# Attention pieces at two places of a dense tile, and the scores of two heads on halves of TensorE's rows

## The chip, the cores and the metric

One core of one Trainium2 chip runs the whole program in one launch. The time is the device time of one execution in microseconds (us); lower is better. The time of the kernel before is 2365.88 us, the median of three runs (2365.64, 2365.88 and 2370.18).

## The reference, cut to what matters

Two layers work on 256 tokens of width 1024. In each layer one input projection feeds three mixers of 8 heads of width 64 each. A is attention with 8 query heads on 2 key heads, with a position bias and learned sinks; B is attention with a cumulative forget bias; C is stick-breaking attention. Their outputs are projected, gated, added and projected once more. A layer ends with an expert stage of 16,384 one-neuron experts.

```python
h = rms_norm(x, norm1_g[l]) * (1.0 + sc1) + sh1
x = x + g1 * parallel_mixers(h, w_in[l], ...)
h = rms_norm(x, norm2_g[l]) * (1.0 + sc2) + sh2
x = x + g2 * peer_ffn(h, w_query[l], ...)
# A: s = q k / 8 - slope * dist, softmax with a sink in the denominator
# B: s = q k / 8 + F[t] - F[s], F = cumsum(log f), causal softmax
# C: beta = sigmoid(q k / 8); A[t,s] = beta[t,s] * prod_{s<j<t} (1 - beta[t,j])
```

## The kernel before

**Weight tiles.** All weights come as a stream of tiles of 128 x 1024 float32, one DMA each (L349), into four buffers `raw`. ScalarE copies a tile to the rounded type fp32r as `hi` (`head`, L445), VectorE computes the rest `lo` = raw - hi (`rest_of`, L751), and TensorE multiplies three times for each of a tile's eight chunks (`product`, L1230 to L1234): hi by mov_hi, hi by mov_lo, lo by mov_hi, 256 columns each. So a tile is 24 matmuls. `rest_of` runs AHEAD = 3 tiles before the tile that TensorE is at; `head` of tile t + 3 waits until tile t - 1 is done (L444).

**The dense stage.** A layer begins with DENSE = 55 tiles: 31 give the queries, keys, values and forget gates of A, B and C, and 24 the merge gates. Results go to two PSUM banks `pj` in turn, from where ScalarE takes them to `projT` (`evict`, L495, L499). The attention of the three mixers is cut into pieces that are issued between these tiles, at numbers written out by hand at L83 to L89. Each engine has its own loop over the tile number t:

- TensorE (L1381 to L1449) issues first all pieces of t and then the tile's 24 matmuls. Pieces are `scores` for one head (L1293; two heads at each t of 8 to 11 for A and of 20 to 23 for B), `turn` (transposes of the probabilities, L1315), `values` (L1324), `logits` of one head of C (L1334), `tails` (L1347), `stick_values` (L1362), and `norms`, `turn_v`, `turn_y`.
- VectorE (L914 to L975) issues first `rest_of` of tile t + 3 and then its pieces: `biased` (L825: two reductions from PSUM at L834 per head), `prob_copy` (L851), `divided` (L860), `normed` (L819), for C `stick_parts` (L875), `stick_arg_of` (L888) and `stick_mask` (L895), and at 24 numbers ADA_AT a `modulation` (L756), a pass over a 512 KB tile of other weights with its own DMA (L357).
- ScalarE (L555 to L596) issues `head` of t + 3, its pieces (`softplus` of C, L518, three passes of 384 columns), and `evict` of t.

Mixer C takes one head at each number of STICK: TensorE does `logits` at t, ScalarE `softplus` at t, VectorE `stick_parts` at t + 1, TensorE `tails` at t + 2 (it waits for L885, the last instruction of `stick_parts`), VectorE `stick_arg_of` at t + 2 and `stick_mask` at t + 3, TensorE `stick_values` at t + 5. Heads use two places of `stick`, and the banks 0, 1 and 2, 3 of `wk`, in turn.

**Scores.** A head's queries and keys lie on 64 partitions: rows 0 to 63 or 64 to 127 of the array. `scores` and `logits` multiply float32 operands, which the profile shows as two matmul passes per instruction. For B the forget bias is added by two fp32r matmuls with 8 rows each (L1311, L1312), after each of the two score matmuls:

```python
for q0, nk, c0 in ((0, P, 0), (P, 2 * P, P)):
    last = pe.matmul(s[:, c0:c0 + nk], q[:, q0:q0 + P], k[:, 0:nk], start=True, stop=br == 0)
    if br:
        pe.matmul(s[:, c0:c0 + nk], pick_f, f_hi[:, 0:nk], start=False, stop=False)
        last = pe.matmul(s[:, c0:c0 + nk], pick_f, f_lo[:, 0:nk], start=False, stop=True)
```

`scores` of a head waits until VectorE has read the head two before (`score_read`), since two banks are used in turn.

Of the kernel before, what the change touches and what calls it, by code (L numbers as in the profile page):

```python
# [20 lines left out]
P = 128  # L21
KC = D // P
HD = 64
# [74 lines left out]
C_ID, C_ONE, C_IOTA, C_ZERO, C_EPS, C_C = 0, 128, 256, 384, 385, 386  # L98
NCONST = 386 + KC
# [5 lines left out]
def trunk(nc, stream, par_dram, const_dram, mix_dram, taba_dram, keys_dram, front_dram, ada_dram, x_dram, out_dram):  # L105
# [4 lines left out]
    with ctx:  # L110
# [19 lines left out]
        picks = sb("picks", [HEADS, HEADS], f32r)  # L130
# [6 lines left out]
        f_pair = routes  # L137
# [75 lines left out]
        f_hi, f_lo = f_pair[0:HEADS, 0, :], f_pair[0:HEADS, 1, :]  # L213
# [58 lines left out]
        f_ready = sem("f_ready")  # L272
        score_ready = sem("score_ready")
# [165 lines left out]
        def _(act):  # L439
# [19 lines left out]
            with act.Fori(0, DEPTH) as l:  # L459
# [95 lines left out]
                for t in range(DENSE):  # L555
# [32 lines left out]
                    if t in STICK:  # L588
                        softplus(STICK.index(t))
                    if t - 2 in STICK:  # L590
                        stick_tail(STICK.index(t - 2))
# [147 lines left out]
        def _(dve):  # L739
# [28 lines left out]
            nc.vector.tensor_copy(picks[:, :], ident[0:HEADS, 0:HEADS])  # L768
# [8 lines left out]
            with dve.Fori(0, DEPTH) as l:  # L777
# [136 lines left out]
                for t in range(DENSE):  # L914
                    rest_of(L0 + (t + AHEAD), t + AHEAD)
# [11 lines left out]
                    if t == SCORE_A + 1:  # L927
# [7 lines left out]
                        link(nc.vector.tensor_scalar(f_hi, fl[:, 2, :], -1.0, None, ALU.mult))  # L935
                        nc.vector.scalar_tensor_tensor(f_lo, fl[:, 2, :], -1.0, f_hi.bitcast(f32), ALU.mult,
                                                       ALU.subtract).then_inc(f_ready, 1)
                    if t == SCORE_A + 3:
                        maxima(0, 1)
                    if TURN_A <= t < TURN_A + 4:  # L940
                        prob_copy(0, 2 * (t - TURN_A))
                        prob_copy(0, 2 * (t - TURN_A) + 1)
# [15 lines left out]
                    if TURN_B <= t < TURN_B + 4:  # L958
                        prob_copy(1, 2 * (t - TURN_B))
                        prob_copy(1, 2 * (t - TURN_B) + 1)  # L960
# [4 lines left out]
                    if t - 2 in STICK:  # L965
# [263 lines left out]
        def _(pe):  # L1229
# [21 lines left out]
            with pe.Fori(0, DEPTH) as l:  # L1251
# [9 lines left out]
                def project(t, j, o, bank, chunks=None, at=range(KC)):  # L1261
# [31 lines left out]
                def scores(br, h):  # L1293
                    n = 8 * br + h

                    if n >= 2:
                        pe.wait_ge(score_read, 16 * l + n - 1)
                    if br == 0:
                        o = (h // 4) * HD
                        q, k = projT[o:o + HD, QA + h % 4, :], projT[o:o + HD, KA, :]  # L1300
                    else:
                        o = (h % 2) * HD
                        q, k = projT[o:o + HD, QB + h // 2, :], projT[o:o + HD, KB + h // 2, :]
                    s = wk[:, 2 + h % 2, :]
                    pick_f = picks[0:HEADS, h:h + 1].to_broadcast([HEADS, P])
# [18 lines left out]
                def values(br, h):  # L1324
                    pe.wait_ge(pt_copied, 16 * l + 8 * br + h + 1)
                    v = (h // 4) * HD if br == 0 else P + h * HD
# [7 lines left out]
                def logits(h):  # L1334
                    if h >= 2:
                        pe.wait_ge(z_read, 8 * l + h - 1)
                    else:

                        pe.wait_ge(score_read, 16 * l + 16)
                    o = (h % 2) * HD  # L1340
# [40 lines left out]
                for t in range(DENSE):  # L1381
# [10 lines left out]
                    if SCORE_A <= t < SCORE_A + 4:  # L1392
                        scores(0, 2 * (t - SCORE_A))
                        scores(0, 2 * (t - SCORE_A) + 1)
                    if VALUE_A <= t < VALUE_A + 4:
                        values(0, 2 * (t - VALUE_A))
                        values(0, 2 * (t - VALUE_A) + 1)
                    if TURN_A <= t < TURN_A + 4:
                        turn(0, 2 * (t - TURN_A))
                        turn(0, 2 * (t - TURN_A) + 1)  # L1400
# [11 lines left out]
                    if t == SCORE_B:  # L1412
                        pe.wait_ge(out_free, l * OUTS + (VB + 4 + 2))
# [15 lines left out]
                    if t == V_C:  # L1429
                        pe.wait_ge(out_free, l * OUTS + (VC + 4 + 2))  # L1430
                        pe.wait_ge(y_read, 3 * l + 2)
                        turn_v(VC, 4, 4)
                    if t == STICK[0]:
                        pe.wait_ge(out_free, l * OUTS + (KCT + 4 + 2))
                    if t == STICK[0] + 5:
                        pe.wait_ge(vtok_in, 3 * l + 3)
                    if t - 5 in STICK:
                        stick_values(STICK.index(t - 5))
# [227 lines left out]
```

## Time and profile before

| what | value |
| --- | --- |
| median of three runs | 2365.88 us |
| the profiled execution, its own time | 2368.43 us |
| span of its instructions | 2366.5 us |
| TensorE matmul busy | 2260.6 us (96%) |
| VectorE busy | 1658.2 us (70%) |
| ScalarE busy | 1225.9 us (52%) |
| mean granted TensorE clock | 0.975 of full speed |
| DMA | 427.46 MB, 181 GB/s in the mean |

PE is TensorE's matmuls, PEld its weight loads, DVE is VectorE, ACT ScalarE, POOL GpSimd, SP SyncE. Matmuls are pipelined: their ends are modelled and their durations overlap, so the time of one is read from start to start. PEclk is the granted clock as a share of full speed: 1.00 is 2.4 GHz, 0.50 is 1.2 GHz. Idle time stands behind the bar or in brackets, with the instruction that ended it.

### The profile page before, as it was taken

The page shows a single profiled execution, that of the slowest core. Times are in us where ns is not written, and L with a number is a line of the kernel's source. Part 1 is how long each engine was busy: PE and PEld are TensorE (multiplying, and loading weights), DVE is VectorE, ACT ScalarE, POOL GpSimd, SP SyncE. Part 2 cuts the span into 40 slices and gives each one's busy share as a digit, 9 for nine tenths or more (in the row PEclk, how much of TensorE's full clock was granted, in tenths as well). Part 3 has the DMA queues.
Part 4 walks back from the last instruction along what each step waited for, and adds up shares of the span by engine and source line. Part 5 has one row for each costly group of instructions (what it writes and reads, how often), then busy time and mean ns, then how long its engine had stood idle before and what let it go on. Part 6 is the DMA issues. An engine that isn't in the chain of part 4 may idle for free.

```text
span 2366.5 us, 45922 instructions
## 1 busy us (share of the span) xinstructions
PE 2260.6 (96%) x15348; PEld 2097.7 (89%) x15348; DVE 1658.2 (70%) x3147; ACT 1225.9 (52%) x2136; POOL 229.6 (10%) x266
## 2 busy tenths in 40 slices
PE   5998998999999999999989999999999999999998
PEld 4888998999999988888878889889999999888887
DVE  6645574788869966777556556738887799567765
ACT  4444545444557755554454445454445677555454
POOL 0000000000037700000000000000001475000000
PEclk7989999999999999999999899999999999999999
DMA  8434553455553357887644345435555433577764
GB/s 320 150 132 165 188 182 125 160 179 185 170 174 110 116 168 239 253 263 229 194 168 156 120 175 190 167 116 178 186 171 193 143 116 107 195 254 254 261 215 160
DMA packets 114451, 427.46 MB, mean 181 GB/s; under 512 B 12704, under 2 KB 12960, under 8 KB 113056
## 3 DMA queue, kind: packets, MB, share of 16 engines
q1 hardware_dynamic: 114336, 426.08, 53.8%
q8 instruction: 54, 0.88, 0.1%
q14 instruction: 61, 0.50, 0.1%
HBM read 424.98 MB, written 1.05 MB: 180 GB/s over the span
## 4 chain that ended last, share of the span: by engine, by line
PE 90%; DVE 3%; issue 3%; ACT 2%; DMA 1%; SPq 0%; ACTq 0%; DVEq 0%
PE pj L1232 17%; PE pj L1233 16%; PE pj L1234 16%; PE wk L1232 10%; PE wk L1234 10%; PE wk L1233 10%; PE wk L1524 5%; PE wk L1307 1%; ACT hi L445 1%; DMA arena<-in_front 1%; PE wk L1494 1%; PE wk L1257 1%; PE wk L1281 0%; PE wk L1343 0%; PE wk L1321 0%
## 5 line engine op out<-in xcount | busy, mean ns | idle before, releaser
L751 DVE TENSOR_TENSOR lo<-raw,hi 128x1024 fp32r<-128x1024 f32 x683 | 839.2, 1230 | 646.3 <-ACT hi L445 637.8
L1232 PE MATMUL pj<-mov_hi,hi 128*128 128x256 f32 x3376 | 993.8, 294 | 39.8 <-DVE mov_lo L802 26.2
L1233 PE MATMUL pj<-mov_lo,hi 128*128 128x256 f32 x3376 | 967.6, 287 | 0.0
L1234 PE MATMUL pj<-mov_hi,lo 128*128 128x256 f32 x3376 | 966.6, 286 | 0.0
L445 ACT ACTIVATE hi<-raw 128x1024 fp32r<-128x1024 f32 x683 | 720.5, 1056 | 454.7 <-PE wk L1234 344.7
L1232 PEld LDWEIGHTS pj<-mov_hi,hi 128*128 128x128 f32 x3376 | 659.2, 195 | 51.7 <-DVE mov_lo L802 28.8
L1233 PEld LDWEIGHTS pj<-mov_lo,hi 128*128 128x128 f32 x3376 | 661.1, 196 | 0.5
L1234 PEld LDWEIGHTS pj<-mov_hi,lo 128*128 128x128 f32 x3376 | 659.8, 195 | 0.0
L1232 PE MATMUL wk<-hi,mov_hi 128*128 128x512 f32 x1024 | 398.6, 389 | 1.7 <-DVE mov_lo L1181 1.7
L1234 PE MATMUL wk<-hi,mov_lo 128*128 128x512 f32 x1024 | 398.4, 389 | 0.0
L1233 PE MATMUL wk<-lo,mov_hi 128*128 128x512 f32 x1024 | 398.3, 389 | 0.0
L433 POOL TENSOR_SCALAR mov_hi<-const,routes 128x128 fp32r<-128x128 f32 x256 | 218.2, 868 | 1188.8 <-DVE gateT L1133 1059.5
L1232 PEld LDWEIGHTS wk<-hi,mov_hi 128*128 128x128 f32 x1024 | 192.2, 188 | 41.9 <-DVE mov_lo L1181 2.1
L1234 PEld LDWEIGHTS wk<-hi,mov_lo 128*128 128x128 f32 x1024 | 192.2, 188 | 39.9
L1233 PEld LDWEIGHTS wk<-lo,mov_hi 128*128 128x128 f32 x1024 | 192.2, 188 | 39.9
L649 ACT ACTIVATE arena<-pj 128x256 f32 (+1 forms) x192 | 73.5, 384 | 276.0 <-PE pj L1234 275.9
L1145 DVE TENSOR_SCALAR onehot_a<-const,routes,gateT 128x128 f32<-128x128 f32 x512 | 147.0, 351 | 0.0
L756 DVE SCALAR_TENSOR_TENSOR arena<-arena,silu_c 128x1024 f32<-128x1024 f32 x88 | 106.4, 1219 | 2.4 <-DMA arena<-in_front 2.2
L1181 DVE TENSOR_TENSOR mov_lo<-arena,mov_hi 128x256 fp32r<-128x256 f32 x256 | 106.5, 417 | 1.1 <-ACT mov_hi L711 1.1
L711 ACT ACTIVATE mov_hi<-arena 128x256 fp32r (+1 forms) x256 | 102.3, 401 | 0.0
L495 ACT ACTIVATE arena<-pj 128x256 f32<-128x256 f32 x62 | 23.8, 383 | 150.5 <-PE pj L1234 150.5
L676 ACT ACTIVATE mov_lo<-const,routes 128x128 fp32r<-128x128 f32 x256 | 81.0, 397 | 0.0
(182 smaller groups left out, 1597.4 us busy)
## 6 DMA issues: line engine op xcount, KB each, us to landing
raw<-in_stream SPq DMA_DIRECT2D x684, 512.0 KB, 3.4
arena<-in_ada SPq DMA_DIRECT2D x72, 512.0 KB, 4.6
onehot_a<-in_ada SPq DMA_DIRECT2D x24, 512.0 KB, 4.6
arena<-in_front SPq DMA_DIRECT2D x4, 2048.0 KB, 18.0
arena<-in_taba SPq DMA_DIRECT2D x2, 1536.0 KB, 19.0
arena<-in_keys SPq DMA_DIRECT2D x2, 1024.0 KB, 4.7
x<-in_xT SPq DMA_DIRECT2D x1, 1024.0 KB, 4.8
arena<-in_mix SPq DMA_DIRECT2D x2, 512.0 KB, 15.2
```

The costliest lines, as they stand in the source:

```text
L433: e = nc.gpsimd.tensor_scalar(onehot_b[0][:, quad % 4 * 2 + r, :], iota, idx2T[:, t:t + 1], None, ALU.is_equal)
L445: nc.scalar.activation(hi[j % SPLIT][:, :], raw[j % RAW][:, :], ACT.Copy).then_inc(hi_done, 1)
L676: e = nc.scalar.activation(onehot_b[1][:, slot + r, :], iota, ACT.Abs, bias=idx2T[:, quad * 4 + r:quad * 4 + r + 1], scale=-1.0)
L711: nc.scalar.activation(w_hi[:, s, :], group_of(n), ACT.Copy).then_inc(w_head, 1)
L751: nc.vector.tensor_tensor(lo[j % SPLIT][:, :], raw[j % RAW][:, :], hi[j % SPLIT][:, :].bitcast(f32), ALU.subtract).then_inc(lo_done, 1)
L756: nc.vector.scalar_tensor_tensor(tile, tile, 1.0, silu_c[:, :], ALU.mult, ALU.mult, accum_out=col)\
L1145: e = nc.vector.tensor_scalar(onehot_a[:, quad % 2 * 4 + r, :], iota, idx1T[:, t:t + 1], gateT[:, t:t + 1], ALU.is_equal, ALU.mult)
L1181: nc.vector.tensor_tensor(w_lo[:, s, :], group_of(n), w_hi[:, s, :].bitcast(f32), ALU.subtract).then_inc(w_rest, 1)
L1232: pe.matmul(out, w_h, m_h, start=first, stop=False)
L1233: pe.matmul(out, w_h, m_l, start=False, stop=False)
L1234: return pe.matmul(out, w_l, m_h, start=False, stop=last)
L1524: last = pe.matmul(wk[:, 2 + quad % 4, :].rearrange("p (i t) -> p t i", t=4)[:, r, :], onehot_a[:, quad % 2 * 4 + r, :], onehot_b[half][:, ...
```

## The change

It gives the pieces two places per tile. In TensorE's loop `early_pieces` go ahead of the tile (norms, scores, tails, logits, transposes of values of A and C and of the outputs), and `late_pieces` after the tile's fourth chunk of eight (turns, values, the transposes of B's values, stick values). In VectorE's loop all pieces but `prob_copy` and `modulation` now stand ahead of `rest_of`. Mixer C takes two heads at each of four numbers of STICK, the second head of a pair one tile behind the first on ScalarE and VectorE, with `stick_values` four tiles behind instead of five. ADA_AT is drawn anew.

`scores` and `logits` take a pair of heads, one on rows 0 to 63 and the other on rows 64 to 127, each to its own bank, and their matmuls stand side by side: both heads' first 128 queries, then both heads' rest. For B the forget bias is added by one fp32r matmul of 64 rows per head and part, where rows 0 to 7 and 64 to 71 of `f_rows` hold the rounded part and rows 32 to 39 and 96 to 103 the remainder, and the other rows are zeros that GpSimd writes. The heads of A are renumbered so that a pair uses both key heads. The layout of weights on the host follows.

```diff
-STICK = (27, 29, 32, 34, 37, 39, 42, 44)
-V_C, Y_C = 31, 50
+STICK = (28, 33, 38, 43)
+V_C, Y_C = 31, 49
 SIGMOID = (47, 49)
-ADA_AT = (5, 13, 14, 16, 18, 19, 22, 24, 25, 27, 29, 31, 32, 34, 36, 39, 41, 42, 44, 46, 48, 49, 51, 53)
+ADA_AT = (5, 13, 14, 18, 20, 21, 22, 24, 25, 26, 27, 31, 32, 33, 36, 37, 41, 42, 46, 47, 50, 51, 52, 53)
...
+                wait_alone(pool, sq_ready, 2 * KC * l + KC)
+                nc.gpsimd.memset(f_rows.bitcast(f32), 0.0).then_inc(f_zero, 1)
...
                 for t in range(DENSE):
-                    rest_of(L0 + (t + AHEAD), t + AHEAD)
+                    for n in range(2):
+                        if t - n - 1 in STICK:
+                            stick_parts(2 * STICK.index(t - n - 1) + n)
+                        if t - n - 3 in STICK:
+                            stick_mask(2 * STICK.index(t - n - 3) + n)
+                    for n in range(2):
+                        if t - n - 2 in STICK:
+                            stick_arg_of(2 * STICK.index(t - n - 2) + n)
...
+                        dve.wait_ge(f_zero, l + 1)
+                        nc.vector.tensor_scalar(f_rows[64:64 + HEADS, :], fl[:, 2, :], -1.0, None, ALU.mult)
+                        link(nc.vector.tensor_scalar(f_rows[0:HEADS, :], fl[:, 2, :], -1.0, None, ALU.mult))
+                        for at in (32, 96):
+                            e = nc.vector.scalar_tensor_tensor(f_rows[at:at + HEADS, :], fl[:, 2, :], -1.0,
+                                                               f_rows[0:HEADS, :].bitcast(f32), ALU.mult, ALU.subtract)
+                        e.then_inc(f_ready, 1)
...
-                    if t - 3 in STICK:
-                        stick_mask(STICK.index(t - 3))
-                    if t - 2 in STICK:
-                        stick_arg_of(STICK.index(t - 2))
-                    if t - 1 in STICK:
-                        stick_parts(STICK.index(t - 1))
...
+                    rest_of(L0 + (t + AHEAD), t + AHEAD)
+                    if TURN_A <= t < TURN_A + 4:
+                        prob_copy(0, 2 * (t - TURN_A))
+                        prob_copy(0, 2 * (t - TURN_A) + 1)
+                    if TURN_B <= t < TURN_B + 4:
+                        prob_copy(1, 2 * (t - TURN_B))
+                        prob_copy(1, 2 * (t - TURN_B) + 1)
                     if t in ADA_AT:
                         modulation(ADA_AT.index(t))
                 rest_of(L0 + (DENSE + AHEAD), DENSE + AHEAD)
...
                         if chunks is not None:
                             pe.wait_ge(mov_ready, l * M_READY + (chunks + k + 1))
+                        if between is not None and k == KC // 2:
+                            between()
                         last = product(pj[bank][:, 0:SEQ], *chunk(j, k), mov_hi[:, at[k], :], mov_lo[:, at[k], :],
...
+                    n = 8 * br + 2 * pair
+                    if n % 8:
+                        pe.wait_ge(score_read, 16 * l + n)
                     for q0, nk, c0 in ((0, P, 0), (P, 2 * P, P)):
-                        last = pe.matmul(s[:, c0:c0 + nk], q[:, q0:q0 + P], k[:, 0:nk], start=True, stop=br == 0)
+                        for h in range(2):
+                            rows = slice(h * HD, (h + 1) * HD)
+                            q = projT[rows, (QA, QB)[br] + pair, q0:q0 + P]
+                            k = projT[rows, KA if br == 0 else KB + pair, 0:nk]
+                            last = pe.matmul(wk[:, 2 + h, c0:c0 + nk], q, k, start=True, stop=br == 0)
                         if br:
-                            pe.matmul(s[:, c0:c0 + nk], pick_f, f_hi[:, 0:nk], start=False, stop=False)
-                            last = pe.matmul(s[:, c0:c0 + nk], pick_f, f_lo[:, 0:nk], start=False, stop=True)
-                    last.then_inc(score_ready, 1)
+                            for h in range(2):
+                                rows = slice(h * HD, (h + 1) * HD)
+                                last = pe.matmul(wk[:, 2 + h, c0:c0 + nk],
+                                                 picks[rows, 2 * pair + h:2 * pair + h + 1].to_broadcast([HD, P]),
+                                                 f_rows[rows, 0:nk], start=False, stop=True)
+                    last.then_inc(score_ready, 2)
...
-                def logits(h):
-                    if h >= 2:
-                        pe.wait_ge(z_read, 8 * l + h - 1)
+                def logits(pair):
+                    if pair:
+                        pe.wait_ge(z_read, 8 * l + 2 * pair)
                     else:
                         pe.wait_ge(score_read, 16 * l + 16)
-                    o = (h % 2) * HD
-                    q, k = projT[o:o + HD, QC + h // 2, :], projT[o:o + HD, KCT + h // 2, :]
-                    z = wk[:, 2 + h % 2, :]
-                    pe.matmul(z[:, 0:SEQ], k[:, 0:P], q, start=True, stop=True)
-                    pe.matmul(z[:, SEQ:SEQ + P], k[:, P:2 * P], q[:, P:2 * P], start=True,
-                              stop=True).then_inc(z_ready, 1)
+                    for n, (q0, nq, c0) in enumerate(((0, SEQ, 0), (P, P, SEQ))):
+                        for h in range(2):
+                            rows = slice(h * HD, (h + 1) * HD)
+                            q, k = projT[rows, QC + pair, q0:q0 + nq], projT[rows, KCT + pair, n * P:(n + 1) * P]
+                            last = pe.matmul(wk[:, 2 + h, c0:c0 + nq], k, q, start=True, stop=True)
+                    last.then_inc(z_ready, 2)
                 def tails(h):
...
+                def early_pieces(t):
...
+                def late_pieces(t):
+                    if VALUE_A <= t < VALUE_A + 4:
+                        values(0, 2 * (t - VALUE_A))
+                        values(0, 2 * (t - VALUE_A) + 1)
+                    if TURN_A <= t < TURN_A + 4:
+                        turn(0, 2 * (t - TURN_A))
+                        turn(0, 2 * (t - TURN_A) + 1)
...
-                        pe.wait_ge(qk_done, 2 * l + 2)
-                        pe.wait_ge(f_ready, l + 1)
-                    if SCORE_B <= t < SCORE_B + 4:
-                        scores(1, 2 * (t - SCORE_B))
-                        scores(1, 2 * (t - SCORE_B) + 1)
...
+                    for n in range(2):
+                        if t - n - 4 in STICK:
+                            stick_values(2 * STICK.index(t - n - 4) + n)
...
+                for t in range(DENSE):
+                    early_pieces(t)
+                    project(L0 + t, t, t, t % 2, None if t else 0, between=lambda: late_pieces(t))\
+                        .then_inc(tile_done, 2 if t == DENSE - 1 else 1)
...
+            if b == "a":
+                wo = wo.reshape(8, HD, D)[qh].reshape(512, D)
```

## Rows read from the trace of the kernel before

**Rows 1.** The page's busy time: us, share of the span, and instructions of each engine.

```profile
PE 2260.6 (96%) x15348; PEld 2097.7 (89%) x15348; DVE 1658.2 (70%) x3147; ACT 1225.9 (52%) x2136; POOL 229.6 (10%) x266
```

**Rows 2.** Waits of TensorE, whole run: us in total, times, longest.

```profile
PE wk L1356 <- DVE arena L885: 22.3, 16, 2.8
...
PE wk L1307 <- DVE arena L822: 3.6, 4, 1.3
PE wk L1377 <- DVE arena L869: 3.2, 2, 1.6
...
PE wk L1329 <- DVE arena L858: 1.4, 2, 0.7
...
PE wk L1290 <- ACT arena L495: 0.9, 2, 0.5
```

**Rows 3.** The dense stages of layers 1 and 2: busy, PEclk, DMA share, GB/s.

```profile
39.50:297.10 257.60, 241.82 (x1764) 227.44 (x1763) 148.09 (x258) 123.84 (x228) 5.59 (x3) 0.94 0.47 160
1204.50:1461.70 257.20, 241.47 (x1766) 227.46 (x1766) 148.86 (x260) 124.28 (x229) 5.60 (x3) 0.94 0.46 160
```

**Rows 4.** Timeline of VectorE, one head of mixer C: start, us, instruction [idle before].

```profile
230.44 1.23 DVE L751 TENSOR_TENSOR lo<-raw,hi 128x1024 fp32r<-128x1024 f32 x1 [2.84 <-ACT hi L445]
...
232.64 0.55 DVE L885 SCALAR_TENSOR_TENSOR arena<-wk,arena 128x384 f32<-128x384 f32 x1
```

**Rows 5.** Stretches at and before a drop of the clock, columns as in rows 3.

```profile
68.90:72.30 3.40, 3.40 (x18) 3.40 (x17) 0.52 (x4) 0.00 (x0) 0.00 (x0) 0.50 0.51 154
126.90:130.30 3.40, 3.40 (x17) 2.28 (x17) 2.25 (x10) 0.02 (x1) 1.07 (x1) 1.00 0.80 301
130.30:133.70 3.40, 3.40 (x19) 3.40 (x18) 0.34 (x2) 0.00 (x0) 0.00 (x0) 0.51 0.67 243
...
1427.40:1430.80 3.40, 1.51 (x13) 1.31 (x13) 3.37 (x6) 1.42 (x2) 0.00 (x0) 1.00 0.40 136
1430.80:1434.20 3.40, 3.40 (x19) 3.40 (x18) 2.31 (x4) 0.53 (x1) 0.00 (x0) 0.50 0.92 320
```

**Rows 6.** Timeline of TensorE, two products of a tile inside 130.30:133.70.

```profile
130.70 0.41 PE L1232 MATMUL pj<-mov_hi,hi 128*128 128x256 f32 x1
130.91 0.41 PE L1233 MATMUL pj<-mov_lo,hi 128*128 128x256 f32 x1
```

**Rows 7.** Timeline of TensorE, one head's `scores` of B and the next head's start.

```profile
143.94 0.50 PE L1307 MATMUL wk<-arena 64*128 64x128 f32 x2
...
145.78 0.37 PE L1307 MATMUL wk<-arena 64*128 64x128 f32 x1
```

**Rows 8.** Timeline of TensorE, two heads' `scores` of A, the tile before, the turns after.

```profile
81.82 0.28 PE L1233 MATMUL pj<-mov_lo,hi 128*128 128x256 f32 x1
81.94 0.28 PE L1234 MATMUL pj<-mov_hi,lo 128*128 128x256 f32 x1
82.14 1.57 PE L1307 MATMUL wk<-arena 64*128 64x128 f32 x8
83.65 0.66 PE L1321 MATMUL wk<-const,arena 128*128 128x128 f32 x4
```

**Rows 9.** Timeline of TensorE, the last `values` of B, `logits` of one head of C.

```profile
174.66 0.39 PE L1330 MATMUL wk<-arena 128*128 128x64 f32 x2
174.88 0.39 PE L1331 MATMUL wk<-arena 128*128 128x64 f32 x2
175.20 0.70 PE L1343 MATMUL wk<-arena 64*128 64x256 f32 x2
...
176.04 0.39 PE L1232 MATMUL pj<-mov_hi,hi 128*128 128x256 f32 x1
```

**Rows 10.** Groups of VectorE's instructions by form in 42:297: busy us, mean ns.

```profile
L756 DVE SCALAR_TENSOR_TENSOR onehot_a<-onehot_a,silu_c 128x1024 f32<-128x1024 f32 x12 | 14.6, 1218 | 0.0
...
L834 DVE CUSTOM_DVE_ANT_0 arena<-wk,arena 128x256 f32<-128x256 f32 x16 | 6.7, 417 | 0.0
```

**Rows 11.** The page's DMA issues: count, KB each, us from issue to landing.

```profile
onehot_a<-in_ada SPq DMA_DIRECT2D x24, 512.0 KB, 4.6
```

More of the change, by code:

```diff
@@ L96 @@
 NPAR = 102
-C_ID, C_ONE, C_IOTA, C_ZERO, C_EPS, C_C = 0, 128, 256, 384, 385, 386
-NCONST = 386 + KC
+C_ID, C_ONE, C_IOTA, C_EPS, C_C, C_PICK = 0, 128, 256, 384, 385, 385 + KC
+NCONST = 385 + KC + HEADS
 X_BLK, X_TRI, X_CM, X_BT = 0, 128, 256, 640
@@ L129, in trunk @@
         silu_c = sb("silu_c", [P, D])
-        picks = sb("picks", [HEADS, HEADS], f32r)
+        picks = sb("picks", [P, HEADS], f32r)
         mod = sb("mod", [P, N_ADA])
@@ L212, in trunk @@
         fl = sq[0:HEADS, 5:8, :]
-        f_hi, f_lo = f_pair[0:HEADS, 0, :], f_pair[0:HEADS, 1, :]
+        f_rows = routes[:, 0, :]
         pj = [ctx.enter_context(nc.psum_tensor(f"pj{i}", [P, 512], f32)) for i in range(2)]
@@ L272, in trunk @@
         f_ready = sem("f_ready")
+        f_zero = sem("f_zero")
         score_ready = sem("score_ready")
@@ L587, in _ @@
                         v_copy(2, wk[:, 4:6, :], P + 512, P + 1024)
-                    if t in STICK:
-                        softplus(STICK.index(t))
-                    if t - 2 in STICK:
-                        stick_tail(STICK.index(t - 2))
+                    for n in range(2):
+                        if t - n in STICK:
+                            softplus(2 * STICK.index(t - n) + n)
+                        if t - n - 2 in STICK:
+                            stick_tail(2 * STICK.index(t - n - 2) + n)
                     if t == SIGMOID[0]:
@@ L767, in _ @@
             dve.wait_ge(setup_loaded, 32)
[L768 removed]
+            nc.vector.tensor_copy(picks[:, :], const[:, C_PICK:C_PICK + HEADS])
             dve.sem_inc(x_ready, KC)
@@ L1259, in squares, with project @@
                         last.then_inc(ss_ready, 1)
-                def project(t, j, o, bank, chunks=None, at=range(KC)):
+                def project(t, j, o, bank, chunks=None, at=range(KC), between=None):
                     pe.wait_ge(lo_done, t + 1)
@@ L1291, in turn_v, with scores @@
                     last.then_inc(vtr, 1)
[L1293 to L1301, printed above, removed]
[L1302 to L1313 removed]
+                def scores(br, pair):
+                    n = 8 * br + 2 * pair
+                    if n % 8:
+                        pe.wait_ge(score_read, 16 * l + n)
+                    for q0, nk, c0 in ((0, P, 0), (P, 2 * P, P)):
+                        for h in range(2):
[3 more added lines that the diff above has]
+                            last = pe.matmul(wk[:, 2 + h, c0:c0 + nk], q, k, start=True, stop=br == 0)
+                        if br:
+                            for h in range(2):
[4 more added lines that the diff above has]
+                    last.then_inc(score_ready, 2)
                 def turn(br, h):
@@ L1379, in turn_y @@
                         last.then_inc(ytr, 1)
-                for t in range(DENSE):
+                def early_pieces(t):
                     if t == NORM_A + 1:
@@ L1392, in _ @@
                     if SCORE_A <= t < SCORE_A + 4:
[L1393 to L1400, printed above, removed]
+                        scores(0, t - SCORE_A)
                     if t == NORM_BQ:
@@ L1412, in _ @@
                     if t == SCORE_B:
+                        pe.wait_ge(qk_done, 2 * l + 2)
+                        pe.wait_ge(f_ready, l + 1)
+                    if SCORE_B <= t < SCORE_B + 4:
+                        scores(1, t - SCORE_B)
+                    if t == V_C:
+                        pe.wait_ge(out_free, l * OUTS + (VC + 4 + 2))
+                        pe.wait_ge(y_read, 3 * l + 2)
+                        turn_v(VC, 4, 4)
+                    for n in range(2):
+                        if t - n - 2 in STICK:
+                            tails(2 * STICK.index(t - n - 2) + n)
+                    if t == STICK[0]:
+                        pe.wait_ge(out_free, l * OUTS + (KCT + 4 + 2))
+                    if t in STICK:
+                        logits(STICK.index(t))
+                    if t == Y_C + 2:
+                        pe.wait_ge(stick_arg, 8 * l + 8)
+                        turn_y(1, 0)
+                    if t == Y_C + 3:
+                        pe.wait_ge(z_read, 8 * l + 8)
+                        turn_y(2, 2)
+                def late_pieces(t):
[5 more added lines that the diff above has]
+                        turn(0, 2 * (t - TURN_A) + 1)
+                    if t == SCORE_B:
                         pe.wait_ge(out_free, l * OUTS + (VB + 4 + 2))
@@ L1428, in _ @@
                         turn(1, 2 * (t - TURN_B) + 1)
[L1429 to L1435, printed above, removed]
-                        pe.wait_ge(vtok_in, 3 * l + 3)
-                    if t - 5 in STICK:
-                        stick_values(STICK.index(t - 5))
-                    if t - 2 in STICK:
-                        tails(STICK.index(t - 2))
-                    if t in STICK:
-                        logits(STICK.index(t))
-                    if t == Y_C + 2:
-                        pe.wait_ge(stick_arg, 8 * l + 8)
-                        turn_y(1, 0)
-                    if t == Y_C + 3:
-                        pe.wait_ge(z_read, 8 * l + 8)
-                        turn_y(2, 2)
-                    project(L0 + t, t, t, t % 2, None if t else 0).then_inc(tile_done, 2 if t == DENSE - 1 else 1)
+                    if t == STICK[0] + 4:
+                        pe.wait_ge(vtok_in, 3 * l + 3)
+                    for n in range(2):
+                        if t - n - 4 in STICK:
[4 more added lines that the diff above has]
+                        .then_inc(tile_done, 2 if t == DENSE - 1 else 1)
                 for n in range(N_BR):
@@ L1618, in _lay_out @@
         q[:, PQP] = i["q_norm_peer"][l]
-        q[:, PSINK:PSINK + 8] = i["sinks"][l]
+        q[:, PSINK:PSINK + 8] = i["sinks"][l][qh]
         q[0:8, PBF] = i["b_forget"][l]
@@ L1639, in _lay_out @@
     taba = np.zeros((P, HEADS, 384), np.float32)
-    for h in range(HEADS):
+    for n, h in enumerate(qh):
         s = 2.0 ** -(h + 1)
         a, b = own - s * d_own, prev - s * d_prev
-        taba[:, h] = np.concatenate([a, b, a], 1)
+        taba[:, n] = np.concatenate([a, b, a], 1)
     keys = np.zeros((DEPTH, P, PEER_HEADS, 256), np.float32)
```

16 lines of the change are left out of this document (3 added, 13 removed).

## The prediction

> **What bounds the kernel now.** The page comes first: TensorE has matmuls in flight 96% of the span, VectorE 70%, ScalarE 52% [rows 1]. So the bound is TensorE's row, and time can leave it in three ways: less work, less idle time, a higher clock. The change touches only the two dense stages, so I read those in the windows: 257.6 and 257.2 us, with VectorE busy 148 to 149 us and ScalarE 124 us [rows 3]. The 55 tiles alone, 24 matmuls each with starts 0.12 us apart [rows 8], are 55 x 2.88 = 158 us. The other 99 us per layer are pieces, idle time and low clock.
>
> The waits of TensorE name the idle time [rows 2]: 22.3 us for `stick_parts` ahead of `tails` (16 times, all heads of C in both layers), 3.6 us for `normed`, 3.2 for `divided`, 1.4 for `prob_copy`, and 0.9 for the eviction of a tile whose values are to be turned. VectorE's timeline shows why [rows 4]: it sat idle 2.84 us until `head` was done, spent 1.23 us on the weight split, and only then began `stick_parts`, whose last instruction starts 2.20 us after the split's start. The pieces stand behind a split that TensorE needs three tiles later.
>
> The clock is the third loss. After a stretch of 3.4 us with only 1.51 us of matmuls the granted clock is 0.50 for the next 3.4 us, and the same follows a stretch that was busy throughout but with `scores` of B [rows 5]. At that level the products start 0.21 us apart instead of 0.12 [rows 6, 8], so of such a stretch a share of 1 - 0.12/0.21 = 0.43 is lost. In the two stages, after their first tile, the clock drops eleven times, first at 68.9 us and last at 1430.8 [rows 5], seven times for 3.4 us and four times for 6.8: 51.2 us. Six drops follow a stretch with idle time (27.3 us, two of them long), the other five a stretch with `scores` of B (23.9 us).
>
> **The change part by part**, as savings against the profiled execution's own 2368.43 us.
>
> *Pieces ahead of the split.* `stick_parts` may now start as soon as ScalarE's logarithms are there, beside the `head` of the same tile, so it uses the 2.84 us in which VectorE idled. It ends some 2.2 us into its tile, and `tails` comes at the next tile, at least 2.88 us after. `normed` and `divided` move ahead of the split likewise and `values` move 12 matmuls (1.44 us) later than the tile's start, more than the waits' 1.3, 1.6 and 0.7 us. So 22.3 + 3.6 + 3.2 + 1.4 = 30.5 us go. The 0.9 us stay: the eviction is bound to the tile's end. What is late next is the second head of a C pair, whose `stick_parts` waits for a `softplus` that itself comes behind `head`; it has 0.5 to 1 us to spare. I allow 2 us of new waits: **28.5 us**, between 20 and 30.5.
>
> What now stands behind these pieces is `rest_of` of t + 3, with the DMA that refills its `raw` buffer (SyncE waits for the split), and the `head` of t + 4. A split that comes 2 to 3 us later still ends some two tiles, over 5 us, ahead of its products. SyncE's queue is passed by nothing new: the modulations' DMAs follow the refills as before. But four modulations stand at 24 to 27 and at 50 to 53. Each one's buffer is refilled after the split one tile earlier and lands 4.6 us later [rows 11], against tiles of 2.9 to 4.9 us, so VectorE can stand still 1 to 2 us there, behind `prob_copy` and behind the split. I cost it at nothing: the cover is the splits' lead. Without it, it would be 2 to 4 us per layer. The same holds for GpSimd's fill of `f_rows` and two more writes of 8 rows on VectorE.
>
> *Drains in B.* One head's `scores` of B take 145.78 - 143.94 = 1.84 us [rows 7], two heads of A 83.65 - 82.14 = 1.51 us [rows 8]. The float32 work is the same, so B's forget bias costs 3.68 - 1.51 = 2.17 us per pair for eight small matmuls. Their columns would be 4 x 0.11 + 4 x 0.12 = 0.92 us. The rest is the change from 64 rows to 8 and back; a change of rows from 128 to 64 shows the same, since `logits` starts at 175.20 where the passes before it end their step at 174.88 + 0.22 = 175.10 [rows 9]. The new form has four bias matmuls per pair of 64 rows, so no change of rows: 1.51 + 0.46 = 1.97 us against 3.68, a saving of 1.71 per pair, for 8 pairs **13.7 us**. If the cost lay in the change between float32 and fp32r, only half the matmuls would be saved, 8 x 0.46 = 3.7 us; that is the lower end.
>
> *Logits.* One head takes 176.04 - 175.10 = 0.94 us [rows 9], two 1.88. A pair in one place has the columns of a pair of A, 1.51. 8 x 0.37 = **3.0 us**.
>
> *Two heads side by side.* No row has two neighbouring matmuls on different halves, so this is bounded: nothing at one end, half of the float32 passes at the other. A head's two passes share their rows and cannot overlap, so of the order 0, 0, 1, 1 each second pass of a head can run beside the first of the other: five steps instead of eight, 0.87 us instead of 1.30 (passes of 0.11 and 0.22 us). The weight loads say the same: passes with 64 columns start 0.11 us apart [rows 9], no faster than passes with 128, so a pass needs 0.11 us for its weights however short it is, and eight make 0.88 us. That is 0.43 us for each of 24 pairs, **10.3 us**. I take it, being nearer to the middle of the bounds, and because the pairs go to two banks.
>
> The Trainium skill ("TensorE: Matmul & The Clock Gate", Part 3) has it that matmuls on different row groups start within about 4 ns of each other. By that rule a pair of heads would cost what one does, and the term would be 24 x 0.65 = 15.6 us; the spacing of the short passes speaks against it.
>
> *Clock.* With the idle stretches gone and the B stretches at most half `scores`, what preceded the drops is no longer there. All of it would be 51.2 x 0.43 = 22.0 us. I keep one drop of 3.4 us: **20.5 us**. The lower end is the part after idle stretches alone, 27.3 x 0.43 = 11.7 us.
>
> *Late pieces inside a tile.* They have 128 rows as the products have, so cutting a tile in two adds no change of rows: nothing. If each of the 19 cuts of a layer cost 0.2 us, it would be 7.6 us in both.
>
> Sum: 28.5 + 13.7 + 3.0 + 10.3 + 20.5 = 76.0 us; 2368.43 - 76.0 = 2292.4. The profiled execution is 2.5 us above the median, so the median would be 2289.9. **I predict 2290 us.**
>
> **The rivals.**
>
> *The halves do not overlap* (0.26). The matmuls stand side by side but run in turn. All other terms stay: 2290 + 10.3 = 2300 us. For it: nothing in the trace shows an overlap. Against it: each half has its own rows and bank.
>
> *The halves overlap in full* (0.08): 2290 - 5.3 = 2285 us, against the load spacing above.
>
> *New waits take the place of the old* (0.14). VectorE's loop is now tied to TensorE's early pieces and to `softplus`; `scores` of the next pair need both heads of the last one read. The Trainium skill ("TensorEngine Tiling (Array Packing)", PSUM Bottleneck) warns of this: packing speeds up TensorE, not the emptying of PSUM. In a tile with `scores` of B VectorE has four reductions of at most 0.42 us, a split of 1.23 and at 20 to 22 a modulation of 1.3 [rows 4, 10], 4.2 us with some waiting, and TensorE 2.88 + 1.5 to 2.0. It is near. If half of the old waits come back in another form (15 us) and with them 6 us of low clock, the time is 2290 + 21 = 2311 us.
>
> *Slower* (0.02). The split becomes what the products wait for. VectorE has pieces ahead of the split at about 37 tiles of a layer. Each would have to make TensorE wait over 76/74 = 1.0 us before the kernel is slower; at 1.2 us the time is 2290 + 89 = 2379 us. Against it: 148 us of work in a stage that would be about 220 us long, and a lead of three tiles.
>
> **How the numbers follow.** My forecast's own case has 0.50: 2282 to 2297 with its terms' bounds. Without overlap it is 2300 to 2308; with the drains or the clock at their lower end (10.0 and 8.8 us less saved) or with new waits 2309 to 2314. The range **2277 to 2314 us** leaves out the slower case and the ends of the new waits. A measurement of this kernel can tell about 0.2% (4.7 us) from no change. Faster by more: 0.97; within: 0.01; slower by more: 0.02.
>
> **What would show it.** In the changed profile, right: the wait for `stick_parts` is gone from TensorE's waits; one pair's `scores` of B take 1.3 to 1.6 us (2.0 without overlap, 3 with the drains kept); a pair of A 0.9 to 1.1 instead of 1.51; dense stages of about 220 us with a mean clock of 0.99. Wrong: products that wait for the split, VectorE's waits for modulation DMAs followed by waits of TensorE, or low clock in stretches without idle time.

## The result and the profile after

The changed kernel takes 2277.36 us, the median of four runs (2275.80 to 2278.94). Against runs of the kernel before, taken beside them, the ratio is 0.9615, with an interval of 0.9596 to 0.9633. Put on the 2365.88 us of the runs shown before, that is 2274.8 us: faster by 91 us, where 76 were forecast, and 2 us below the range of 2277 to 2314. A second set of runs gave 2279.78 us and 0.9621 (0.9590 to 0.9651), which is within 2 us of the first. Both intervals reach over the lower edge of the range, but neither reaches the 76 us that were forecast.

The page's busy line and the waits of TensorE after the change, to be held against [rows 1] and [rows 2]:

```profile
PE 2201.6 (97%) x15316; PEld 2053.9 (90%) x15316; DVE 1661.9 (73%) x3151; ACT 1223.8 (54%) x2136; POOL 232.5 (10%) x268
```

```profile
PE pj L1241 <- DVE mov_lo L805: 25.3, 8, 16.9
...
PE wk L1513 <- DVE arena L1044: 7.0, 2, 3.5
...
PE pj L1241 <- DVE mov_lo L1010: 4.5, 2, 2.3
...
PE pj L1241 <- DVE arena L998: 3.0, 2, 1.5
...
PE wk L1301 <- ACT arena L497: 0.9, 2, 0.5
```

Of the five waits of [rows 2] only the last is left, the eviction, with the same 0.9 us; 30.5 us are gone. What still stands here was there before and lies at the start of a layer or behind the dense stage. Work on VectorE is as before; it is TensorE's busy time that shrank too.

The two dense stages, from the first product to the end of the last tile, before and then after (columns as in [rows 3]):

```profile
37.10:297.20 260.10, 244.28 (x1772) 229.67 (x1772) 150.59 (x264) 125.26 (x230) 5.59 (x3) 0.94 0.47 162
1202.10:1461.70 259.60, 243.31 (x1772) 228.91 (x1772) 150.57 (x264) 125.27 (x230) 5.60 (x3) 0.94 0.47 163
```

```profile
37.30:251.30 214.00, 213.53 (x1756) 207.51 (x1756) 151.11 (x266) 124.53 (x230) 6.75 (x3) 0.99 0.57 196
1157.20:1371.00 213.80, 212.81 (x1756) 206.31 (x1756) 151.26 (x266) 124.53 (x230) 6.74 (x3) 0.99 0.57 196
```

They are 46.1 and 45.8 us shorter, together 91.9; the rest of the kernel is 1 us longer. The mean clock rose from 0.94 to 0.99, and what is missing to 1.00 lies in the first tile: none of the eleven drops came back. TensorE stands idle for only 0.5 and 1.0 us of them.

TensorE's timeline of two heads' `scores` of A and of B after the change, against [rows 8] and [rows 7]:

```profile
66.11 0.93 PE L1314 MATMUL wk<-arena 64*128 64x128 f32 x8
66.97 0.38 PE L1241 MATMUL pj<-mov_hi,hi 128*128 128x256 f32 x1
...
117.02 0.49 PE L1314 MATMUL wk<-arena 64*128 64x128 f32 x4
117.27 0.31 PE L1319 MATMUL wk<-routes,picks 64*128 64x128 f32 x2
117.41 0.65 PE L1314 MATMUL wk<-arena 64*128 64x256 f32 x4
117.71 0.47 PE L1319 MATMUL wk<-routes,picks 64*128 64x256 f32 x2
118.11 0.39 PE L1241 MATMUL pj<-mov_hi,hi 128*128 128x256 f32 x1
```

A pair of A takes 66.97 - 66.11 = 0.86 us where it took 1.51, a pair of B 1.09 us where two heads took 3.68. The eight passes of a pair of A start at 66.111 and 66.117, 66.324 and 66.331, 66.436 and 66.442, 66.654 and 66.661 us: two by two, 6 to 7 ns apart, one for each half of the rows.

Taken from start to start of TensorE's matmuls and summed over both stages, idle time apart, the 92 us split so: idle time 32.1 to 1.5 us (30.6 saved), products 350.5 to 333.0 (17.5, nearly all of it the clock), `scores` 42.8 to 15.5 (27.3), `logits` 15.0 to 6.8 (8.2), `tails` 17.5 to 13.0 (4.5), `stick_values` 11.2 to 9.4 (1.8), the rest 2.2.

### The profile page after: what moved, and what is told of

Same layout as the page of the kernel before. It is cut to its first block, busy times and chain, and to the rows that moved or that the text cites. A ratio compares the mean times of both kernels' runs of the same rounds, so it can differ in the third digit from the quotient of the medians.

```text
span 2275.8 us, 45868 instructions
## 1 busy us (share of the span) xinstructions
PE 2201.6 (97%) x15316; PEld 2053.9 (90%) x15316; DVE 1661.9 (73%) x3151; ACT 1223.8 (54%) x2136; POOL 232.5 (10%) x268
## 4 chain that ended last, share of the span: by engine, by line
PE 95%; DVE 1%; ACT 1%; DMA 1%; issue 1%; SPq 0%; ACTq 0%; DVEq 0%
PE pj L1241 18%; PE pj L1242 17%; PE pj L1243 17%; PE wk L1241 10%; PE wk L1242 10%; PE wk L1243 10%; PE wk L1543 5%; DMA arena<-in_front 1%; PE wk L1513 1%; PE wk L1314 1%; PE wk L1266 1%; PE wk L1292 0%; PE wk L1330 0%; PE wk L1339 0%; PE wk L1340 0%
## 5 line engine op out<-in xcount | busy, mean ns | idle before, releaser
L1241 PEld LDWEIGHTS pj<-mov_hi,hi 128*128 128x128 f32 x3376 | 649.8, 192 | 51.8 <-DVE mov_lo L805 28.8
L1242 PEld LDWEIGHTS pj<-mov_lo,hi 128*128 128x128 f32 x3376 | 651.7, 193 | 0.5
L1243 PEld LDWEIGHTS pj<-mov_hi,lo 128*128 128x128 f32 x3376 | 650.7, 193 | 0.0
## 6 DMA issues: line engine op xcount, KB each, us to landing
arena<-in_front SPq DMA_DIRECT2D x4, 2048.0 KB, 18.1
arena<-in_mix SPq DMA_DIRECT2D x2, 512.0 KB, 15.3
```

Of the source, the lines that this page charges most:

```text
L1241: pe.matmul(out, w_h, m_h, start=first, stop=False)
L1242: pe.matmul(out, w_h, m_l, start=False, stop=False)
L1243: return pe.matmul(out, w_l, m_h, start=False, stop=last)
```

## The experiments

Each kernel was run beside runs of the kernel before; the ratio is to those. Each edit is made to the changed kernel unless said otherwise. Two kernels of different sets are best compared by their ratios, since medians of one kernel can differ by 2 us from set to set (2277.36 and 2279.78 above).

**e1: both heads of a pair on the same rows.**

```diff
-                            rows = slice(h * HD, (h + 1) * HD)
+                            rows = slice(0, HD)
```

(at the three places where `scores` and `logits` choose rows; the second head of a pair is then computed from the first one's operands)

> The changed kernel with both heads of a pair on rows 0 to 63, so that no two neighbouring score matmuls stand on different halves (the second head then computes with the first one's operands, so its scores are not the reference's). Theory, full overlap: in the changed profile the two heads' passes start 7 ns apart and a pair costs 0.86 us (A), 0.85 (C), 1.09 (B). Without the overlap it should cost 1.51, 1.51 and 1.97, so 0.65 + 0.66 + 0.88 = 2.19 us more per three pairs, 17.5 us in all: 2295 us. Rival, partial overlap as I predicted (five steps of eight): 10.3 us, 2288 us. Rival, the starts shown are modelled and the halves do not really overlap: no change, 2277 us.

Measured: 2295.75 us, ratio 0.9685 (0.9666 to 0.9704). TensorE's timeline:

```profile
66.36 1.57 PE L1314 MATMUL wk<-arena 64*128 64x128 f32 x8
67.87 0.39 PE L1241 MATMUL pj<-mov_hi,hi 128*128 128x256 f32 x1
```

A pair of A is back at 1.51 us with the same eight passes, a pair of B at 1.97, a pair of C at 1.50. Summed over both stages `scores` went from 15.5 to 27.8 us and `logits` from 6.8 to 12.0: 17.4 us more, where full overlap said 17.5 and my own five steps of eight 10.3. The whole is 18.4 us slower by the medians and 16.6 by the ratios; with intervals of some 4 us on each ratio the total alone would not tell 17.5 from 10.3, the timeline does. TensorE's waits in the dense stages stayed as in the changed kernel, and so did the clock, but for 3 us of low clock in the second tile of layer 2. So the halves overlap in full.

**e6: the same matmuls, one head after the other.**

```diff
-                    for q0, nk, c0 in ((0, P, 0), (P, 2 * P, P)):
-                        for h in range(2):
+                    for h in range(2):
+                        for q0, nk, c0 in ((0, P, 0), (P, 2 * P, P)):
```

(and the same in `logits`)

> The changed kernel with the same matmuls of a pair, on the same halves and banks, but in another order: all of the first head, then all of the second. Theory, a matmul only runs beside its neighbour in the order of issue: a pair of A or C then overlaps at most where the heads meet (0.1 to 0.2 us), so most of the 17.5 us is lost: 2290 to 2295 us. Rival, what matters is the half alone and TensorE takes the second head's passes forward: no change, 2277 us.

Measured: 2281.16 us, ratio 0.9625 (0.9600 to 0.9650).

```profile
66.51 0.93 PE L1314 MATMUL wk<-arena 64*128 64x128 f32 x8
67.37 0.38 PE L1241 MATMUL pj<-mov_hi,hi 128*128 128x256 f32 x1
```

The theory fell. A pair of A still takes 0.86 us, although four passes of the first head are issued ahead of the second's. Its passes start at 66.507 and 66.521, 66.721 and 66.734 (the four of 128 columns), then 66.832 and 66.846, 67.051 and 67.064 us (the four of 256): 14 ns apart, the second head's short passes ahead of the first head's long ones. Only B's pair grew, to 118.86 - 117.45 = 1.41 us in this kernel's timeline; why, no run shows. Over both stages `scores` and `logits` take 2.7 us more. So for A and C it is enough that the two heads have different halves; they need not be neighbours. With B's bias matmuls between them the order does matter, by 0.32 us a pair.

**e4: the bias matmuls of B on 8 rows.**

```diff
-                                rows = slice(h * HD, (h + 1) * HD)
+                                rows = slice(h * HD, h * HD + HEADS)
...
-                                                 picks[rows, 2 * pair + h:2 * pair + h + 1].to_broadcast([HD, P]),
+                                                 picks[rows, 2 * pair + h:2 * pair + h + 1].to_broadcast([HEADS, P]),
```

> The changed kernel with B's forget-bias matmuls on 8 rows instead of 64 (rows 0 to 7 and 64 to 71; the remainder of the bias, in the rows left out, is not added). Count, columns and place of the matmuls are the same, only their number of rows changes. Theory, the drains of the kernel before came from the change of the row count: four changes per pair at 0.1 to 0.2 us each, 3 to 6 us over 8 pairs: 2280 to 2284 us, and a pair of B takes 1.5 to 1.9 us in the trace instead of 1.09. Rival, they came from the change between float32 and fp32r or from the two extra matmuls: no change, 2277 us, and a pair takes 1.09 us.

(A drain is here the extra time that TensorE takes where the number of rows changes. This kernel leaves out the remainder of the bias.)

Measured: 2282.14 us, ratio 0.9627 (0.9602 to 0.9652).

```profile
116.70 0.49 PE L1314 MATMUL wk<-arena 64*128 64x128 f32 x4
117.12 0.32 PE L1319 MATMUL wk<-routes,picks 8*128 8x128 f32 x2
117.38 0.70 PE L1314 MATMUL wk<-arena 64*128 64x256 f32 x4
118.01 0.38 PE L1319 MATMUL wk<-routes,picks 8*128 8x256 f32 x2
118.32 0.39 PE L1241 MATMUL pj<-mov_hi,hi 128*128 128x256 f32 x1
```

The total alone would not decide: it is 2 to 5 us above the two sets of the changed kernel. The timeline does. A pair takes 118.32 - 116.70 = 1.62 us instead of 1.09, 4.2 us over 8 pairs, with the same count, columns and types. The change of the number of rows is what costs. The theory counted four changes per pair, but the step to the products' 128 rows is in both kernels, so there are three more (64 to 8, back, and to 8 again): 0.53 / 3 = 0.18 us each. The kernel before had seven inside a pair, and what its 3.68 us hold beside the columns is 3.68 - 1.51 - 0.92 = 1.25 us by the prediction's count, again 0.18 us each. The Trainium skill ("TensorEngine Tiling (Array Packing)", Key Properties) says that changing the tiling mode drains TensorE; the rows agree. No drop of the clock came back in the dense stages here.

**e9: B's matmuls twice, without changes of rows** (on top of e1, so its scores are not the reference's either).

```diff
-                    for q0, nk, c0 in ((0, P, 0), (P, 2 * P, P)):
+                    for q0, nk, c0 in ((0, P, 0), (P, 2 * P, P)) * (1 + br):
```

> The kernel with both heads on rows 0 to 63 (2295.8 us, no drop of the clock in the dense stages beyond the first tile), with all of B's score and bias matmuls issued twice into the same banks, so that a tile with scores of B again has about 3.7 us of them, as long as in the kernel before, but without changes of the row count. Open: why the clock dropped after stretches that were busy with scores of B. Theory, the drains did it, four changes of the row count per head: no drop comes back, only the work, 8 x 1.8 us: 2310 us. Rival, it was the score passes themselves (64 rows, float32) that keep the clock down: four to six drops come back around B's scores, 6 to 15 us more, 2317 to 2325 us.

Measured: 2308.94 us, ratio 0.9755 (0.9725 to 0.9785). The stretches with all of B's `scores`, in both layers (columns as in [rows 3]):

```profile
119.30:152.00 32.70, 32.70 (x244) 30.79 (x243) 16.48 (x50) 12.92 (x35) 1.29 (x1) 1.00 0.42 147
1255.70:1288.00 32.30, 32.30 (x240) 30.43 (x240) 16.07 (x49) 12.92 (x35) 1.25 (x1) 1.00 0.41 147
```

A tile had 3.73 us of `scores` (119.35 to 123.08 us in its timeline), as many as before the change, and the granted clock stayed at 1.00 throughout. In the kernel before it fell five times around them. The time grew by 13 us against e1, near the doubled work of 8 x 1.76 = 14.1 us. So 64-row and float32 passes do not bring the clock down by themselves. What is left is what this kernel lacks and the one before had: matmuls of 8 rows and the changes of rows around them. The two are not told apart, and e4, with three such changes in a pair where the kernel before had seven, had no drop either. That the drains did it is argued, not shown.

**e5: VectorE's order alone, put into the kernel before.**

```diff
                 for t in range(DENSE):
-                    rest_of(L0 + (t + AHEAD), t + AHEAD)
                     if t == NORM_A + 2:
...
+                    rest_of(L0 + (t + AHEAD), t + AHEAD)
                     if t in ADA_AT:
```

(with `prob_copy` moved behind `rest_of`)

> The kernel before with one edit alone: VectorE's pieces ahead of the weight split, but prob_copy and modulation behind it, as in the changed kernel; STICK, ADA_AT, scores and TensorE's loop as before. Theory: the 30.6 us of waits in the dense stages go nearly all, and with them the six drops of the clock that followed idle time (11.7 us), but not the five that followed scores of B (10.3 us): 38 to 43 us faster than the kernel before, a ratio of 0.982 to 0.984. Rival, the numbers of STICK are too near for it and waits stay: under 20 us. Rival, the drops of the clock do not follow from the idle stretches: 30 us.

Measured: 2319.67 us, ratio 0.9797 (0.9776 to 0.9818), 48 us faster than the kernel before beside it (2367.43). All four waits are gone. Three drops of the clock are left in the stages, each after `scores` of B:

```profile
120.70:124.10 3.40, 3.40 (x16) 2.09 (x15) 1.07 (x6) 1.23 (x2) 0.11 (x1) 0.99 0.87 304
124.10:127.50 3.40, 3.40 (x17) 3.40 (x17) 1.78 (x5) 0.00 (x0) 0.00 (x0) 0.50 0.17 25
141.10:144.50 3.40, 3.40 (x21) 2.49 (x20) 1.43 (x5) 2.31 (x7) 0.00 (x0) 1.00 0.44 154
144.50:151.30 6.80, 6.80 (x28) 5.81 (x28) 3.20 (x10) 0.76 (x4) 0.00 (x0) 0.50 0.19 58
...
1284.60:1291.40 6.80, 6.80 (x29) 5.81 (x29) 3.12 (x10) 0.68 (x4) 0.00 (x0) 0.50 0.19 64
```

The gain is above the expected 38 to 43 us. 34.1 us of low clock went instead of 27.3, because not every stretch with `scores` of B is followed by a drop. With 30.6 us of waits and 34.1 x 0.43 = 14.7 of clock that is 45 us. The interval of the ratio, 43 to 53 us, holds it. The four executions spread from 2316.84 to 2325.15 us and the trace is of the fastest; whether the others had more drops no trace shows.

**e2: VectorE's split first again, and e7: also TensorE's late pieces ahead of the tile.**

```diff
                 for t in range(DENSE):
+                    rest_of(L0 + (t + AHEAD), t + AHEAD)
                     for n in range(2):
...
-                    rest_of(L0 + (t + AHEAD), t + AHEAD)
                     if TURN_A <= t < TURN_A + 4:
```

> The changed kernel with VectorE's weight split back at the head of its loop, all else kept (two places on TensorE, pairs). Theory, the order on VectorE is what removed the waits: stick_parts again ends over 4 us into its tile and the tails at the start of the next tile but one wait 1 to 2 us, so 15 to 30 us of TensorE waits come back and with them 5 to 12 us of low clock: 2297 to 2319 us. Rival, the waits went because pairs and new numbers gave more room, and TensorE's late place: under 5 us, at most 2282 us.

Measured for e2: 2301.57 us, ratio 0.9714 (0.9697 to 0.9732).

```profile
PE wk L1366 <- DVE arena L888: 11.2, 8, 1.4
...
PE wk L1314 <- DVE arena L825: 5.4, 4, 1.4
...
PE wk L1387 <- DVE arena L872: 3.2, 2, 1.6
...
PE wk L1314 <- DVE small L837: 2.9, 2, 1.5
```

The 24 us are these waits, 22.7 us. The theory's other half, low clock, did not return. No wait behind the first tile of a stage is over 1.6 us here, while five of the six drops behind idle time in the kernel before followed waits of 1.89 and 2.81 us. But the length of a wait does not decide alone. The first drop there, at 68.9 us, followed one of 1.27 us; a wait of 1.26 us at the same place brought none here; and three waits of 1.89 us brought none there, as in the second pair of lines:

```profile
66.96 0.48 PE L1307 MATMUL wk<-arena 64*128 64x128 f32 x2 [1.27 <-DVE arena L822]
65.50:68.90 3.40, 2.13 (x13) 1.56 (x12) 3.39 (x9) 2.58 (x5) 0.00 (x0) 1.00 0.46 154
...
220.39 0.38 PE L1356 MATMUL wk<-arena 128*128 128x128 f32 x1 [1.89 <-DVE arena L885]
217.00:227.00 10.00, 8.11 (x65) 7.66 (x64) 7.12 (x10) 4.46 (x9) 0.00 (x0) 1.00 0.43 160
```

What else it takes stays open.

> The changed kernel with both placements undone (VectorE's split first, TensorE's late pieces ahead of the tile), so that pairs alone are left. With the split first alone it took 2301.6 us, with 22.7 us of new waits and no drop of the clock in the dense stages beyond their first tile. Theory, the late place on TensorE covers what VectorE does behind the split: now values, stick_values and the transposes of B wait too, 5 to 10 us more and perhaps one drop of the clock: 2305 to 2315 us. Rival, the late place is of no use in either order, as it was worth only 3 us in the other: 2302 to 2305 us.

Measured for e7: 2301.32 us, ratio 0.9712 (0.9686 to 0.9737), the same as e2, with the same waits. The rival was right, though the time is 0.7 us under its 2302 to 2305.

**e3: the late pieces ahead of the tile, VectorE as changed.**

```diff
-                    project(L0 + t, t, t, t % 2, None if t else 0, between=lambda: late_pieces(t))\
+                    late_pieces(t)
+                    project(L0 + t, t, t, t % 2, None if t else 0)\
```

> The changed kernel with the late pieces issued ahead of the tile, right after the early ones, all else kept. Theory, the late place only covers prob_copy and the eviction ahead of B's transposes: 2 to 4 us of waits come back (values on L861, stick_values, turn_v), 2279 to 2282 us. Rival, splitting a tile costs something that the profile hides (0.1 to 0.2 us for each of 38 cuts): 4 to 8 us faster, 2270 us. Rival, the late place carries a large part: 10 us slower or more.

Measured: 2280.39 us, ratio 0.9625 (0.9608 to 0.9642). The number falls into the theory's range, but hardly for its reason. Of the waits it named one came back, `values` on `prob_copy` (L861), with 0.7 us in two places; 2 to 4 us were named. The dense stages are 0.3 and 0.5 us longer than in the changed kernel, and the two sets of that kernel differ by 2.4 us themselves. TensorE's late place is worth about 1 us or nothing.

**e8: the same order in the next stage.** In the branch tiles VectorE's gate multiplication and addition stand ahead of `rest_of`.

```diff
                         t = L0 + br * 4 + (T_BR + j)
-                        rest_of(t + AHEAD, j + AHEAD)
...
                         dve.wait_ge(br_add, n + 1)
+                        rest_of(t + AHEAD, j + AHEAD)
```

> The changed kernel with the same idea in the next stage: in the twelve branch tiles behind the dense stage VectorE multiplies by the gates and adds ahead of the weight split instead of behind it. TensorE waits 3.0 us there for that multiplication, 1.5 us in each layer. Theory: the wait goes, 2 to 3 us faster, 2274.5 us. Rival, VectorE is the bound in this stage (2.6 us of work per tile of 2.88 us) and the wait moves to the split or the last addition: within 1 us.

Measured: 2280.95 us, ratio 0.9618 (0.9597 to 0.9640), no gain. The 3.0 us on the multiplication left the waits, and the wait on the last splits of the merged branches grew from 4.5 to 6.4 us:

```profile
PE pj L1241 <- DVE mov_lo L1010: 6.4, 2, 3.2
```

**a1: the changed kernel again.**

> The changed kernel once more, on the same chip as the next run, as its base: 2277 us within 4 us, 0.9615 of the kernel before.

Measured: 2279.78 us, ratio 0.9621 (0.9590 to 0.9651). No version tried beats the changed kernel.

## Why the prediction was right or wrong

The sign, the bound and all mechanisms but one held. The size was too small: 76 us forecast, 91 measured. The step that failed is the overlap of two heads, and a few smaller terms erred to the same side. Both kinds of pair came out below what I had named as signs of being right: 1.09 us for B against 1.3 to 1.6, 0.86 for A against 0.9 to 1.1.

- *Pieces ahead of the split*, forecast 28.5 us: 30.6. Nothing of the 2 us allowed for new waits came. Modulations of three and four tiles in a row did make VectorE wait for their DMAs, 6.9 us in the first stage. This row is the third of three, and TensorE had no wait there:

```profile
177.36 1.23 DVE L759 SCALAR_TENSOR_TENSOR arena<-arena,silu_c 128x1024 f32<-128x1024 f32 x1 [1.31 <-DMA arena<-in_ada]
```

  The splits' lead covered it, as costed. That VectorE's order is the cause e5 shows (the order alone removed the four waits) and e2 (undone, 22.7 us of waits came back).
- *Two heads side by side*, forecast 10.3 us: this is the step that failed. I wrote that "a head's two passes share their rows and cannot overlap", so five steps of eight, and that the weight loads gave the same bound. Both took TensorE for one queue. The two halves ran as two streams: each pass of one head beside the same pass of the other, and their weight loads too, which start 7 ns apart in the trace. The bias matmuls of B, for which I had no overlap at all, ran so as well. The term is 8 x (0.65 + 0.66 + 0.88) = 17.5 us, and the timeline of e1 has 17.4. I had named full overlap as a rival, but with a chance of 0.08 and 5.3 us more instead of 7.1. The rule of the Trainium skill that I set aside ("TensorE: Matmul & The Clock Gate", Part 3) has starts about 4 ns apart and was nearly right; here they are 6 to 7 ns. Its companion, that matmuls keep the program's order, does not describe e6, in which the second head's short passes started ahead of the first head's long ones.
- *Drains in B* (13.7) and *logits* (3.0): with the overlap taken off, `scores` and `logits` saved 35.5 - 17.4 = 18.1 us, of which 2.8 us are what low clock cost these pieces before, so 15.3 us against 16.7. The change of rows is the cause (e4), not that of type. `tails` and `stick_values`, which I put at nothing, saved 6.3 us together: about 2.1 us where a 128-row pass is followed by `logits` of 64 rows (0.205 us to the next start, where the products follow after 0.031 and 0.084), 2.7 us next to the old waits, which the wait rows do not count (a first pass takes 0.10 us more after a wait, a last one is counted to its modelled end), and the rest mostly clock.
- *Clock*, forecast 20.5 us of 22.0: no drop stayed. The products alone saved 17.5 us, the rest, some 4 us, is in the pieces' sums. That drops follow stretches with `scores` of B I read rightly, and e9 shows that their 64-row passes are not the reason. What a stretch with idle time needs for a drop, beside the wait, I did not find (e2).
- *Late pieces inside a tile*: nothing, as costed, and nothing gained either (e3, e7).

Of the 15 us by which I was short, 7.1 are the overlap, 2.1 the waits, about 1.3 the clock, and about 5 the steps of `tails` and `stick_values`; the drains came 1.4 us smaller, the rest 2 us larger. Together that is 16 us, 1 us more than the 15. The order alone gives 48 us (e5), the pairs with the new numbers 69 (e7, 2370.77 to 2301.32), both 91: each removes some of the same waits and drops. What the new numbers of STICK and ADA_AT are worth by themselves was not run.

## What to carry to other kernels

Where an engine works ahead for another, put what that other needs now in front of what it needs three steps later: that reorder alone gave 2%. Put small matmuls of 64 rows on both halves of the array, as here in different banks, and keep the number of rows the same from one to the next, even if zero rows must be added. Then look at the clock row again: here low clock followed stretches with waits and stretches with 8-row matmuls, so both cost a second time. Where a term rests on an overlap that no row shows, give full overlap its price and its chance: here it was the largest miss.

## What the runs showed of the hardware

Two float32 matmuls on different row halves ran fully in parallel, starts 6 to 7 ns apart, and still did, 14 ns apart, when the second was issued four passes after the first (e6). A change between 64 and 8 rows cost about 0.18 us, three in a pair in e4 and seven in the kernel before. The granted clock stayed at 2.4 GHz through tiles with 3.73 us of 64-row `scores` (e9), but fell to 1.2 GHz after stretches with the same work broken by 8-row matmuls (five times in the kernel before, three in e5, never in e4, which has fewer). It stayed up through all waits of up to 1.6 us in e2, and fell after waits of 1.9 and 2.8 us in the kernel before, but there also after one of 1.27 us, and not after three of 1.9.
